# One region for the opening, the sample chunk, the ring and the branch merge

## The reference

```
ada = silu(c) @ w_ada + b_ada                  # six sections: shift, scale, gate, twice
h   = rmsnorm(x) * (1 + scale1) + shift1
q|f|i|g|b|c|v = h @ w_in                       # seven parts of 512 columns
A:  o = recurrence(silu(q), f, i, state)       # 4 heads of 128 x 128; exact per token
    y_a = (rmsnorm(o) * silu(g)) @ w_pa
B:  y_b = (b * conv3(c * v)) @ w_pb
ga, gb = sigmoid(h @ w_bgate)                  # two halves
x1  = x + gate1 * rmsnorm((ga * y_a + gb * y_b) @ w_o)
h2  = rmsnorm(x1) * (1 + scale2) + shift2
y   = x1 + gate2 * rmsnorm((silu(conv3(gate half of h2 @ w_up)) * other half) @ w_down)
```

## Time and profile before

| | us |
|---|---|
| three timed runs, median (lowest to highest) | 1842.33 (1842.29 to 1842.51) |
| the profiled execution | 1839.17 |
| its span, first to last instruction | 1837.5 |
| TensorE matmuls busy | 1760.5 |
| TensorE weight loads busy, beside them | 1657.3 |
| VectorE busy | 845.1 |
| POOL busy | 533.2 |
| ScalarE busy | 418.8 |
| mean granted TensorE clock, share of 2.4 GHz | 0.979 |

### The profile page before, as it was taken

One profiled execution on the slowest core, in us unless ns is written; L12 is line 12 of the kernel. 1 busy time (PEld: TensorE's weight loads), 2 busy tenths in 40 slices (PEclk: granted clock), 3 DMA queues, 4 the chain that ended last, 5 costly groups with the idle time before them and its releaser, 6 DMA issues.

```text
span 1837.5 us, 24923 instructions
## 1 busy us (share of the span) xinstructions
PE 1760.5 (96%) x9865; PEld 1657.3 (90%) x9865; DVE 845.1 (46%) x1027; ACT 418.8 (23%) x596; POOL 533.2 (29%) x256
## 2 busy tenths in 40 slices
PE   4899898999998999999899999999999999999996
PEld 2898898999998999999688999999999999999994
DVE  5520233676764001322345554545545456456456
ACT  4331311333333112000444212011011110111203
POOL 1523323111111332332352422213223133133224
PEclk9899989999999999999899999999999999999998
DMA  9364232312111111110423201011020110210204
GB/s 362 140 233 139 101 99 76 97 54 62 47 41 40 35 51 59 55 51 17 139 90 115 69 24 57 23 57 46 23 68 16 52 57 13 67 46 23 91 24 164
DMA packets 145610, 139.06 MB, mean 76 GB/s; under 512 B 4643, under 2 KB 130834, under 8 KB 142482
## 3 DMA queue, kind: packets, MB, share of 16 engines
q1 hardware_dynamic: 142530, 126.49, 21.5%
q10 hardware_dynamic: 3024, 11.80, 1.6%
HBM read 116.99 MB, written 19.19 MB: 74 GB/s over the span
## 4 chain that ended last, share of the span: by engine, by line
PE 49%; DVE 1%; issue 1%; ACT 0%; DMA 0%; POOLq 0%; POOL 0%; ACTq 0%
PE p_up L184 29%; PE p_down L2163 14%; PE p_m L2092 5%; PE p_up L2135 1%; PE p_m L2116 1%; DVE middle L2070 1%; PE p_x1T L2103 0%; DVE middle L2039 0%; DMA q<-w_o 0%; POOLq L1720 0%; DVE w_o_halves L1952 0%; POOL wup_halves L170 0%; ACT w_o_halves L1870 0%; DVE mlp_hidden L2033 0%; DVE gate_conv L2026 0%
## 5 line engine op out<-in xcount | busy, mean ns | idle before, releaser
L184 PE MATMUL p_up<-h,wup_halves 128*128 128x384 f32 x3024 | 526.3, 334 | 0.7 <-POOL wup_halves L170 0.7
L184 PEld LDWEIGHTS p_up<-h,wup_halves 128*128 128x128 f32 x3024 | 524.7, 188 | 1.8 <-POOL wup_halves L170 1.0
L2163 PE MATMUL p_down<-w_down_halves,mlp_hidden 128*128 128x512 f32 x1188 | 274.5, 391 | 6.4 <-DVE mlp_hidden L2033 3.4
L2163 PEld LDWEIGHTS p_down<-w_down_halves,mlp_hidden 128*128 128x128 f32 x1188 | 222.6, 189 | 55.7 <-DVE middle L2039 6.9
L170 POOL TENSOR_TENSOR wup_halves<-wup_raw,wup_halves 128x1024 fp32r<-128x1024 f32 x42 | 118.5, 2822 | 356.0 <-ACT wup_halves L165 356.0
L184 PE MATMUL p_mix<-h,ws_halves 128*128 128x384 f32 x1152 | 205.1, 337 | 9.5 <-SPq L123 6.4
L184 PEld LDWEIGHTS p_mix<-h,ws_halves 128*128 128x128 f32 x1152 | 202.6, 190 | 10.6 <-issue 10.6
L155 POOL TENSOR_TENSOR ws_halves<-ws_raw,ones 128x1024 fp32r<-128x1024 f32 (+1 forms) x48 | 80.3, 1674 | 395.9 <-PE p_mix L184 176.1
L184 PE MATMUL p_ring<-h,ws_halves 128*128 128x384 f32 x864 | 174.2, 349 | 5.0 <-SPq L123 5.0
L2039 DVE TENSOR_TENSOR middle<-middle,p_down 128x512 f32<-128x512 f32 x180 | 123.3, 687 | 108.5 <-PE p_down L2163 105.6
L184 PEld LDWEIGHTS p_ring<-h,ws_halves 128*128 128x128 f32 x864 | 150.1, 191 | 8.6 <-POOL ws_halves L158 5.3
(11 more groups left out here) (261 smaller groups left out, 1832.8 us busy)
## 6 DMA issues: line engine op xcount, KB each, us to landing
wup_raw<-w_up SPq DMA_DIRECT2D x42, 512.0 KB, 3.9
w_ada_slice<-w_ada SPq DMA_DIRECT2D x16, 1024.0 KB, 7.4
ws_raw<-w_in SPq DMA_DIRECT2D x28, 512.0 KB, 4.2
w_down_raw<-w_down SPq DMA_DIRECT2D x11, 1024.0 KB, 6.0
w_ada_first<-w_ada SPq DMA_DIRECT2D x8, 1024.0 KB, 17.6
ws_raw<-w_bgate SPq DMA_DIRECT2D x16, 512.0 KB, 3.9
k_logf_v_scratch<-middle ACTq DMA_DIRECT2D x12, 576.0 KB, 2.8
x_after_mixer_scratch<-x_tile_mid SPq DMA_DIRECT2D x9, 512.0 KB, 2.6
```

Of the source, the lines that this page charges most:

```text
L184: last = pe.matmul(out[:, 0:G], self.halves[:, s, a, kt * P:(kt + 1) * P], moving[:, b, kt, g * G:(g + 1) * G], start=(j == 0 and kt == 0) ...
L2163: last = pe.matmul(pdn[:, half, :], ff[:, a, f, t * P:(t + 1) * P], wd[:, b, f, half * HALF:(half + 1) * HALF], start=(j == 0 and f == 0), ...
```

## The change

The first four regions become one. The five engine bodies of each are now functions (`qfi_sync`, `g_sync`, `ring_sync`, `mix_sync` and so on), and in one `nc.Block` every engine runs its four functions one behind the other. What the boundaries ordered is now ordered by waits on single semaphores, in the diff below. The two calls of `new_semaphores` inside go, and one comes in behind the merge, ahead of the last region; the w_o loads of the merge therefore count on kept names (`late_wo_in`).

PSUM has one layout for all: the two banks of the ada products become the readout and the shared bank, the three banks of projection slot 0 become the ring (for g too), and the three of slot 1 become `work`: levels even, levels odd (and the gates' rows), tokens. The merge uses `work` and the ring as its two slots. In SBUF the buffers of the sample chunk and of the convolution are now allocated beside those of the recurrence.

The last `ada_transposes` move from the end of the opening into the first g product, behind its fourth run, and all steps of the sample chunk come two runs later in g. SP loads the sample states as soon as the buffers of f are free, then the chunk when its scratch writes have landed; before the ring it loads chunk 1 ahead of chunk 0. SP's starting counts of the merge and the sample chunk, nine, are given at the very start; those of g's and the ring's banks are no longer needed. Two loads of ScalarE's table go. Apart from indentation the diff is, cut:

```diff
-            with nc.Block() as block:
-                @block.sync
-                def _(sp):
+            def qfi_sync(sp):
...
-                        ada_transposes(i + 2)
+                    if first:
+                        ada_transposes(2)
...
-        pl = pb(rec, "p_levels", [P, 2, HW // 2])
-        pt = pb(rec, "p_tokens", [P, 512])
         po = pb(rec, "p_readout", [P, 512])
         px = pb(rec, "p_shared", [P, 512])
+        ring = pb(rec, "p_ring", [P, NG, 512])
+        work = pb(rec, "p_levels_and_tokens", [P, NG, 512])
+        pl = work[:, 0, :].rearrange("p (two n) -> p two n", two=2)
+        pl_odd, pt = work[:, 1, :], work[:, 2, :]
...
-        new_semaphores()
...
-                    start_at_one(sp, ["s_" + n for n in CHUNK_STARTS] + [f"g_ring{g}" for g in range(NG)])
-                    load_chunk(sp, "s_", 0, 0, slice(NP_, T), None)
+        def g_sync(sp):
+            sp.wait_ge(sem("f_k"), H)
+            sp.wait_ge(sem("f_done"), H)
             for b in range(NB):
                 sp.dma_start(heads(S0[b]), io["state_hgrn"][0, b].rearrange("h k v -> k h v")) \
                     .then_inc(sem("s_S0"), 16)
+            sp.wait_ge(sem("ada_done"), SLICES + 2 * KD)
+            for dst, n, written in ((Kc, 0, "k_out"), (R, 1, "f_out"), (Vc, 2, "v_out")):
+                sp.wait_ge(sem(written), 16 * H)
+                sp.dma_start(heads(dst[:, 0, :]), kfv_scratch[n, :, :, NP_:T]).then_inc(sem("s_in0"), 16)
...
+            def last_ada_columns():
+                pe.wait_ge(sem("ada_rows"), 3)
+                pe.wait_ge(sem("ada_sum"), 4)
+                for i in range(4):
+                    last = pe.transpose(pcolumns[:, i * P:(i + 1) * P], arow[:, i * P:(i + 1) * P], ident[:, :])
+                last.then_inc(sem("ada_T"), 1)
...
-                    steps = {2: gate_rows, 6: "in", 7: 0, 9: 1, 10: 2, 12: 3, 14: "kd", 16: "o", 32: "ms"}
-                    steps.update({18 + 3 * b // 2: f"state{b}" for b in range(NB)})
+            steps = {3: last_ada_columns, 6: gate_rows, 8: "in", 9: 0, 11: 1, 12: 2, 14: 3, 16: "kd", 18: "o", 34: "ms"}
+            steps.update({20 + 3 * b // 2: f"state{b}" for b in range(NB)})
...
-                        ws.product(pe, U0 + n // 2, n % 2, KD, h, lambda g: (gring[:, g, :], f"g_ring{g}", n + 1), between)
+                ws.product(pe, U0 + n // 2, n % 2, KD, h, lambda g: (ring[:, g, :], *((f"ring{g}", n) if n else ("qfi_pfree0", U0 + 1))), between)
...
-                    load_prompt_chunk(0)
             load_prompt_chunk(1)
+            load_prompt_chunk(0)
...
+            pool.wait_ge(sem("s_fin"), 3)
             no_decay(0)
             no_decay(1)
...
-        new_semaphores()
...
-            ps = [pb(ctx, f"p_mix{s}", [P, NG, 512]) for s in range(2)]
+        pmix = [work, ring]
...
-                    act.wait_ge(sem("late_prompt_state"), 16)
+            act.wait_ge(sem("p_state"), H * CHUNKS)
             for k in range(H):
+                for g in range(NG):
+                    act.wait_ge(sem(f"ring{g}"), H + 3 * k + 3)
                 act.activation(branch[:, 0, k, :], TM[:, k, :], ACT.Copy).then_inc(sem("branch_hi"), 1)
...
+        with nc.Block() as block:
+            @block.sync
+            def _(sp):
+                start_at_one(sp, ["mix_pfree0", "mix_pfree1", "mix_z"])
+                start_at_one(sp, ["s_" + n for n in CHUNK_STARTS])
+                qfi_sync(sp)
+                g_sync(sp)
+                ring_sync(sp)
+                mix_sync(sp)
...
         mixer.close()
+        new_semaphores()
```

More of the change, by code:

```diff
@@ new lines, in g_scalar, with g_out, g_between @@
+        def g_scalar(act):
+            def g_out(m):
+                hd, g = m // NG, m % NG
+                ws.arrived(act, U0 + hd // 2, hd % 2, g)
+                act.activation(SG[:, hd, g * G:(g + 1) * G], ring[:, g, 0:G], ACT.Copy) \
+                    .then_inc(sem(f"ring{g}"), 1)
+            def g_between(l):
+                for m in range(SLEVELS, 10) if l == SLEVELS else (l,):
+                    g_out(m)
+            chunk_act(act, "s_", 0, 0, SLEVELS, g_between)
+            for m in range(10, NG * H):
+                g_out(m)
@@ new lines, in tokens, with loaded, pair_view, decays_of @@
+        def tokens(c):
+            return slice(c * P, (c + 1) * P)
+        def loaded(eng, c):
+            eng.wait_ge(sem(f"p_in{c % 2}"), (c // 2 + 1) * 64)
+        def pair_view(whole, first, step, inner):
+            return bass.AP(whole.tensor, first, [[whole.ap[0][0], P], [step, 2], *inner])
+        def decays_of(c, l):
+            hh, at = 1 << l, c % 2 * 2 * HW
+            n = HW >> (l + 1)
+            moved = pair_view(RL[:, :, :, :], at + HW, hh - HW, [[2 * hh, n], [1, hh]])
+            ends = pair_view(RL[:, :, :, :], at + 2 * hh - 1, -hh, [[2 * hh, n], [0, hh]])
+            return moved, ends
@@ L1620, in build_trunk @@
-        mixer.close()
+                update(c, 5)
+                operands(c, 5)
+                take(c, 3)
+                if not first and not last:
+                    for n in (1, 3, 4):
+                        conv[n]()
+                update(c, 6)
+                operands(c, 6)
+                take(c, 4)
+                take_diagonal(c)
+                if not first and not last:
+                    for n in (2, 5):
+                        conv[n]()
+                    histories(j)
+                    b_out(j, 0)
@@ new lines, in mix_gpsimd, with mix_tensor, turn @@
+        def mix_gpsimd(pool):
+            with pool.Fori(1, 2 * KD, 1) as j:
+                ws.split(pool, j + U_MIX, 0, KD)
+                ws.split(pool, j + U_MIX, 1, H)
+        def mix_tensor(pe):
+            for n, (_, _, u0) in enumerate(HALVES):
+                def turn(j):
+                    local = j + n * KD
+                    ws.product(pe, j + u0, 0, KD, h, two_slots(pmix, "mix", local, 0))
+                    if isinstance(j, int):
+                        pe.wait_ge(sem("branch_lo"), (n + 1) * H)
+                    ws.product(pe, j + u0, 1, H, branch, two_slots(pmix, "mix", local, 1))
+                turn(0)
+                with pe.Fori(1, KD, 1) as j:
+                    turn(j)
```

1762 lines of the change are left out of this document (852 added, 910 removed), and 14 rows, old and new, of the table RUNS.

## The result

The changed kernel takes 1823.62 us (median of 4 runs, 1822.01 to 1824.22) against 1842.42 for the kernel before on the same chip: a ratio of 0.9899, 95% interval 0.9883 to 0.9915. 1827.3 was forecast. The profiled execution went from 1839.17 to 1822.01 us, 17.2 less, where the sum said 15.0.

The account below looks back on a forecast made before the run. TensorE bounds the kernel, so time comes only from its stills and half clock; 4.9 + 7.1 + 4.6 - 1.4 - 0.2 = 15.0 us takes the median from 1842.33 to 1827.3, range 1816.5 to 1835.5.

Parts of the forecast that it names:

- Opening to g: First boundary and sample chunk: 8.0 us from idle and clock, 1.6 at state products, less 3.2 and 1.5 at level 0.
- stays as it is: Sample readouts in g: the half-clock stretch from 264.6 to 277.6 at 0.50 was to remain, with the same products.
- The lock: Sample level 0 and merge: POOL and two-SBUF-input VectorE operations exclude each other for a whole instruction; waits 3.2 and 2.5 us.
- g to ring: Second boundary: idle of 4.96 us goes and 2.1 is gained up to the ring's first level, 7.1 in all.
- Ring to merge: Third boundary: 6.4 us of idle and 1.4 of clock gained, 2.5 of wait and 0.7 of clock lost, 4.6 in all.
- Merge to the output projection: Last boundary: the semaphore clearing moves here, ahead of w_o, and costs 1.4 us; 3.0 if priced per semaphore.
- Start: Kernel start: SP makes nine more increments before its first load, costing 0.2 us, ends 0 and 0.5.
- the clock gives nothing back: Rival at all three boundaries: narrow steps and first levels pull the clock down anyhow; 1832.9 us, chance 0.14.
- the stills come back: Rival: TensorE's idles return as waits of single semaphores at two of three places; 1840 us, chance 0.06.
- half clock through the sample chunk: Slower rival: clock falls after level 0 and stays down to the end of g, costing 27 us; 1854, chance 0.05.
- No collisions: Rival at sample level 0 and merge: VectorE and POOL miss each other, 7.9 us more gained; 1819.4, chance 0.25.
- signs of being wrong: The forecast is wrong if a named wait exceeds 5 us or half clock appears anywhere but at the readouts.

Follow-up runs that it names:

- the controls: The changed kernel run twice more with nothing edited: 1828.35 us (ratio 0.9923) and 1826.25 us (0.9928).
- bar_ring: The changed kernel with one plain barrier put back between g and the ring: 1832.17 us, ratio 0.9947.
- one_range: The changed kernel with kept semaphores allocated first, so the 135 cleared ones adjoin in one stretch, not eight: 1823.35 us, ratio 0.9893.
- the two edits: The changed kernel with POOL's split held behind the sample levels' products (1821.72 us), or VectorE's Q-gate product held behind POOL's split (1822.75 us).
- best_spread: The changed kernel with both collisions removed, cleared semaphores adjoining, and the sample's readouts spread behind four runs of g: 1813.78 us, ratio 0.9857.

## Why the prediction was right, and where not

The forecast was 3.7 us above the median and its range held it. Beside the kernel before on their own chips, the three sets of runs of the change are 18.8, 14.0 and 14.2 us faster, and 15.0 was forecast. That it came so near is in part luck, because two steps missed in opposite directions. By its own steps, profile against profile:

*Opening to g: 4.9 foreseen, 9.3 measured.* The still of 5.92 went as a whole; the first runs gained 2.2 of clock (2.1 foreseen); level 0 waits 2.81 (3.2); the state products gained 1.1 (1.6). The step that failed is the clock: 1.5 was charged behind level 0, and the execution paid nothing there and had a half-clock stretch at the readouts that was 2.9 shorter. Both are chance: the same instructions took 78.1 to 84.3 us in this stage, by the clock alone. The "stays as it is" for the readouts was a statement about one execution. 1.6 more came from the opening, which the controls show to be chance.

*The lock* was right in kind and place, and the experiments show it from both ends: each of the two waits went when the split and the two-input operations were kept apart. Which comes first was a close thing at level 0 (POOL at 234.68, VectorE at 234.73), though the wait of 2.81 came in every run without a barrier ahead of g in which POOL was not held back. The Trainium skill ("SBUF — State Buffer", section "SBUF: two separate sides") says that whoever starts first keeps the port pair for the whole instruction; the rows above agree in both directions, POOL first (0.42 becomes 2.13) and VectorE first (1.89 becomes 5.70). The later one is held and not slowed alongside: VectorE's product takes 4.96 with POOL's half waiting beside it, as it did before, when that half began 0.4 before its end; and the half of 1.89 ends 1.75 behind the product.

*g to ring: 7.1 foreseen, 7.3 measured* (19.26 us from "ms" to level 0 before, 9.16 after, two runs of 1.40 fewer), with a new wait of 0.27 (0.5 foreseen) already counted; another 0.4 was gained from there to the merge. The order of the loads cost nothing; bar_ring shows that this hung on the early issue.

*Ring to merge: 4.6 foreseen, 3.6 measured.* 6.43 of idle gained, and 1.0 on the first product (1.4), which took 13.04 at a granted clock of 1.00 and not 12.64: one matmul at its start took 0.73 for 0.33, why stays open; 2.02 lost to POOL's split (2.5) and 1.7 to the clock behind it (0.7). The last was a mean of what turned out to be two cases: behind this idle of 2.0 the product took 14.3 us in four of the profiles and 12.7 to 12.8 in three.

*Merge to the output projection: 1.4 lost foreseen, 4.0 measured.* 2.36 is the clearing (6.10 instead of 3.74 of idle, in every kernel with eight stretches): the term was mis-sized, as I took the price of 64 in five stretches for 135 in eight. The other 1.6 is the wait for the second half's weights and the clock behind it, 3.25 us instead of 3.04 and 15.51 for the product behind it instead of 14.09.

*Start: 0.2 lost foreseen.* TensorE's first product came 0.65 later (8.33 for 7.68), but it did not set the opening's end. The last stage lost 1.1, where nothing had been foreseen: its last products began at half clock, which cost 1.4 behind the same idle of 3.38 as before.

The rivals: "the clock gives nothing back" and "the stills come back" are ruled out by the timeline after, "half clock through the sample chunk" too (behind level 0 it cost 3.0 at most, in one_range, and not 27). "No collisions" is what the two edits make of the kernel.

By the letter, two of the prediction's signs of being wrong came true: the wait ahead of w_o is over 5 us (6.10, of which 3.74 was there before), and half clock appears away from the readouts, behind the wait ahead of the third merge product (granted clock 0.63 from 565.4 to 570.0), for which the sum itself had charged 0.7. And the upper end of the range is not the sum it is said to be: 1832.9 and 3.4 make 1836.3, not 1835.5.

What is left open: which of the lengths the clock takes behind an idle of 2 to 3 us, and at the readouts, no run here lets me foretell.

## What to carry to other kernels

Taking out a barrier pays twice, in the idle, most of which is the tail of another engine's work, and in the clock behind it. But it also moves work that the barrier had kept apart: look for POOL work that reads SBUF beside VectorE operations with two SBUF inputs, and put one wait between them. Count what a barrier's clearing does, and allocate what is kept in one block, so that the cleared numbers adjoin. Where two executions of the same instructions differ by 6 us in one stage, compare stages and not totals, and do not book one execution's clock as a term.

## What was not expected of the hardware

The readouts, 64 matmuls of 16 columns and eight of 128 back to back, bring TensorE to half clock though it is busy all the time: from 265.0 to 278.5 in one_range the granted clock was 0.50 (1.2 GHz), with every us busy (length of the window, busy us of PE, PEld, VectorE, ScalarE and POOL, clock, DMA share, GB/s):

```profile
265.00:278.50 13.50, 13.50 (x57) 13.50 (x58) 1.09 (x2) 1.41 (x4) 0.00 (x0) 0.50 0.13 39
```

With eight wide matmuls between two heads it did not come (best_spread, one profiled execution). Without them the stretch and the wide runs behind it took 3 us more than at full clock in seven executions, 4.7 in one and 6 in four (8.05 + 3.04 us is full clock, four heads of 2.01 and 16 wide matmuls), with no difference in the instructions. The Trainium skill ("TensorE: Matmul & The Clock Gate", section "Part 1: The HAM clock gate (the 'warmup' mystery)") says that the count of slow matmuls at a start varies from run to run; here the same holds in the middle of a kernel, by 3 us a stretch.
